# Later modulation chunks: every second one as float32 products with two moving columns on the tensor engine, the others by the vector engine alone

## The reference

```
silu_ctx = silu(c_ctx)[None]
silu_c = silu(c)
for l in range(2):
    sh_ap, sc_ap, gt_ap, sh_mp, sc_mp, gt_mp = split(silu_ctx @ ada_w[l] + ada_b[l], 6)
    sh_as, sc_as, gt_as, sh_ms, sc_ms, gt_ms = split(silu_c @ ada_w[l] + ada_b[l], 6)
    h = rms_norm(x, norm_mix_pre[l]) * (1 + sc_a) + sh_a
    ... mixer(h @ w_in[l]) ... gated residual with gt_a ... MLP with sh_m, sc_m, gt_m ...
```

## Time and profile before

| | us |
|---|---|
| three runs, median (lowest to highest) | 3354.6 (3351.59 to 3357.12) |
| the profiled execution, its own time | 3357.79 |
| its span, first to last instruction | 3356.1 |
| in-projection 0 beside the later chunks | about 113 to 403 of the span |
| mean granted TensorE clock over the span | 0.941 |

### The profile page before, as it was taken

How to read it: one execution, slowest core, us unless ns; L and a number is a source line. 1 busy time by engine, 2 the same in 40 slices (tenths; PEclk the granted TensorE clock), 3 DMA queues, 4 the chain that set the end, 5 groups by cost and what they waited for, 6 DMA issues and landing times.

```text
span 3356.1 us, 44680 instructions
## 1 busy us (share of the span) xinstructions
PE 3071.4 (92%) x17804; PEld 2687.3 (80%) x17804; DVE 1997.9 (60%) x2685; ACT 1183.4 (35%) x1884; POOL 1203.0 (36%) x705
## 2 busy tenths in 40 slices
PE   7999878999889999999998899857789999999998
PEld 3888646899768999978887898646668999988886
DVE  3699579555477644455555555477777644455555
ACT  2333234555453322211113476543253323211112
POOL 1466336100022544344341221145443544444341
PEclk9999979999899999999999999966689999999999
DMA  5565544000032232332521332321132232333421
GB/s 200 191 215 194 179 129 137 33 26 1 10 110 78 93 107 88 128 121 94 149 80 51 123 129 72 132 80 43 35 111 77 93 107 97 125 116 101 142 80 57
DMA packets 211326, 347.01 MB, mean 103 GB/s; under 512 B 18696, under 2 KB 110896, under 8 KB 211120
## 3 DMA queue, kind: packets, MB, share of 16 engines
q1 hardware_dynamic: 211120, 344.16, 30.8%
HBM read 259.18 MB, written 84.94 MB: 103 GB/s over the span
## 4 chain that ended last, share of the span: by engine, by line
PE 70%; DVE 15%; POOL 6%; issue 4%; ACT 3%; DMA 1%; SPq 1%; POOLq 1%; DVEq 0%; ACTq 0%
PE psum L1044 21%; PE psum L1022 17%; PE psum L692 6%; PE psum L2195 4%; PE psum L695 3%; DVE ada_acc L298 3%; PE psum L1368 3%; PE psum L2183 2%; PE psum L2190 2%; PE psum L2495 2%; DVE mix_x L2678 1%; PE psum L463 1%; DVE mix_v L2691 1%; PE psum L2841 1%; PE psum L1395 1%
## 5 line engine op out<-in xcount | busy, mean ns | idle before, releaser
L1044 PE MATMUL psum<-WF,H 128*128 128x512 f32 x3024 | 691.0, 391 | 11.2 <-POOL WF L1098 11.2
L1044 PEld LDWEIGHTS psum<-WF,H 128*128 128x128 f32 x3024 | 571.1, 189 | 130.7 <-POOL WF L1098 11.6
L1231 DVE TENSOR_TENSOR yacc<-yacc,psum 128x512 f32<-128x512 f32 x468 | 321.8, 688 | 314.7 <-PE psum L1044 314.7
L1022 PE MATMUL psum<-AT,w_slot 128*128 128x288 f32 x2688 | 366.0, 295 | 4.7 <-POOL w_slot L987 4.7
L1022 PEld LDWEIGHTS psum<-AT,w_slot 128*128 128x128 f32 x2688 | 359.5, 188 | 5.1 <-POOL w_slot L987 5.1
L1094 POOL TENSOR_TENSOR H<-pass_a,H 128x2304 fp32r<-128x2304 f32 x32 | 165.7, 5180 | 449.5 <-ACT H L1083 449.5
L692 PE MATMUL psum<-WT,AT 128*128 128x512 f32 (+1 forms) x1296 | 286.0, 381 | 4.2 <-ACT stage L738 4.2
L1083 ACT ACTIVATE H<-pass_a 128x2304 fp32r<-128x2304 f32 x32 | 68.2, 2132 | 596.8 <-PE psum L1044 573.2
L1022 PE MATMUL psum<-s_hi,w_slot 128*128 128x288 f32 x1344 | 269.1, 295 | 5.9 <-issue 4.3
L692 PEld LDWEIGHTS psum<-WT,AT 128*128 128x128 f32 x1296 | 234.4, 192 | 48.6 <-ACT stage L738 4.4
L628 POOL TENSOR_TENSOR WT<-RAW,WT 128x1024 fp32r<-128x1024 f32 (+3 forms) x34 | 114.8, 3401 | 346.3 <-ACT WT L617 346.3
(11 more groups left out here) (396 smaller groups left out, 5384.6 us busy)
## 6 DMA issues: line engine op xcount, KB each, us to landing
RAW<-ffn_w SPq DMA_DIRECT2D x64, 1024.0 KB, 6.3
ada_raw<-ada_w SPq DMA_DIRECT2D x18, 2048.0 KB, 8.2
pass_a<-hidden SPq DMA_DIRECT2D x64, 576.0 KB, 5.1
hidden<-hid SPq DMA_DIRECT2D x56, 576.0 KB, 3.3
RAW<-w_in_even SPq DMA_DIRECT2D x5, 2048.0 KB, 8.3
RAW<-w_in_odd SPq DMA_DIRECT2D x5, 2048.0 KB, 7.9
mix_x<-x_all SPq DMA_DIRECT2D x18, 512.0 KB, 3.6
feat_even<-stage SPq DMA_DIRECT2D x36, 256.0 KB, 5.1
```

What stands on the lines that cost most here:

```text
L1022: mm = nc.tensor.matmul(psum[:, bank + b, 0:HB], w_slot[p][:, w, k, :], TOKENS[p][x][:, k, b * HB:(b + 1) * HB], start=(begins and k == 0 ...
L1044: mm = nc.tensor.matmul(psum[:, DOWN_BANK[n % 8], :], H1[:, g % 2, a, m, (u // 2) * P:(u // 2 + 1) * P], w2[b][:, m, (u % 2) * 512:(u % 2 ...
L1231: tt(y, y, x, add).then_inc(dn_kept, 1)
```

## The change

Even slots and odd slots go different ways.

- **Odd slots** (1, 3, ..., 17): no DVE, ACT or POOL work on the block. PE takes the raw float32 weights themselves as the stationary operand, block by block of 128 x 128, and the two columns of `silu_c` (both vectors) as the moving one: 4 column blocks x 8 pieces = 32 float32 products with two moving columns, summed in PSUM.
- **Even slots** (0, 2, ..., 16): DVE does all eight pieces for both vectors, 16 instructions; PE makes the same 8 products with one column of ones as before.
- ACT's scaling and POOL's adding are gone, with their buffer and semaphores. `ada_acc` is now double-buffered over even slots.
- **Loads**: an odd block is loaded whole after PE's products of the odd slot before; an even block in two halves, each after DVE has read that half of the even slot before. `loads_at` places them in SP's list between the units' outputs, 0.68 of a 512-column unit behind the products of slot q - 2 for an odd slot, and 0.63 of a unit ahead of them and at them for the halves of an even one.
- DVE's order is: products of slot q (even), then `ada_keep` of q - 2 and q - 1.

The places of the products in PE's list stay as they were. The core of the diff:

```
+        def on_pe(q):
+            return q % 2 == 1
+
+        def ada_load(sp, q, h):
             l, at = slot_source(q)
-            sp.dma_start(slot_raw(q)..., ada_v[l][:, :, at:at + 512]).then_inc(ada_in[q % 2], 16)
+            rows = slot_raw(q).rearrange("p (k n) -> p k n", k=KD)
+            if on_pe(q):
+                sp.wait_ge(ada_sum[1], q // 2)
+                sp.dma_start(rows, ada_v[l][:, :, at:at + 512]).then_inc(ada_whole_in, 16)
+            else:
+                if q >= 2:
+                    sp.wait_ge(ada_part, 2 * KD * (q // 2 - 1) + KD * (h + 1))
+                sp.dma_start(rows[:, 4 * h:4 * h + 4, :], ada_v[l][:, 4 * h:4 * h + 4, at:at + 512]).then_inc(ada_in[h], 16)
 
         def ada_latent(dve, q):
+            e, raw = q // 2, slot_raw(q)
+            if e >= 2:
+                dve.wait_ge(ada_sum[0], e - 1)
+            for k in range(KD):
+                if k % 4 == 0:
+                    dve.wait_ge(ada_in[k // 4], 16 * (e + 1))
+                for who in range(2):
+                    acc, w, c = ada_acc[:, e % 2, who, :], raw[:, k * 512:(k + 1) * 512], silu_c[:, k, who:who + 1]
+                    if k:
+                        dve.wait_ge(ada_part, 2 * KD * e + 2 * k + who - 1)
+                        nc.vector.scalar_tensor_tensor(acc, w, c, acc, ALU.mult, ALU.add).then_inc(ada_part, 1)
+                    else:
+                        nc.vector.tensor_scalar(acc, w, c, None, ALU.mult).then_inc(ada_part, 1)
+
+        def ada_products(pe, q):
+            s, e = q % 2, q // 2
+            pe.wait_ge(ada_kept[s], e)
+            if on_pe(q):
+                pe.wait_ge(ada_whole_in, 16 * (e + 1))
+            else:
+                pe.wait_ge(ada_part, 2 * KD * (e + 1))
+            for m in range(4):
+                at = 256 + 2 * m
+                if on_pe(q):
+                    for k in range(KD):
+                        mm = nc.tensor.matmul(psum[:, 6 + s, at:at + 2], slot_raw(q)[:, k * 512 + m * P:k * 512 + (m + 1) * P], silu_c[:, k, :], start=(k == 0), stop=(k == KD - 1))
                 else:
+                    for who in range(2):
+                        mm = nc.tensor.matmul(psum[:, 6 + s, at + who:at + who + 1], ada_acc[:, e % 2, who, m * P:(m + 1) * P], ones[:, 0:1], start=True, stop=True)
             mm.then_inc(ada_sum[s], 1)
...
-        def ada_scalar(act, q, k):
-        def ada_gpsimd(pool, q):
...
+        def loads_at(c, u):
+            t0 = sum(unit_cost(cc) * units(cc) for cc in range(1, c)) + unit_cost(c) * u
+            t1 = t0 + unit_cost(c)
+            done = lambda q: FIRST_PRODUCT + PRODUCT_EVERY * (q - 2)
+            loads = [(done(q) + 370, q, 0) if on_pe(q) else (done(q) - 340 * (1 - h), q, h) for q in range(2, SLOTS) for h in range(1 if on_pe(q) else 2)]
+            return [(q, h) for t, q, h in sorted(loads) if t0 <= t < t1]
...
-            for q in range(SLOTS):
+            for q in range(0, SLOTS, 2):
                 ada_latent(dve, q)
                 if q:
+                    ada_keep(dve, q - 2)
                     ada_keep(dve, q - 1)
-            ada_keep(dve, SLOTS - 1)
+            for q in range(SLOTS - 2, SLOTS):
+                ada_keep(dve, q)
...
-                    for n in pieces_at(c, u):
-                        ada_scalar(act, n // (KD - K_DVE), K_DVE + n % (KD - K_DVE))
```

More of the change, by code:

```diff
@@ L138, in trunk @@
         ada_acc = Region(gate_row_at, AT0)("ada_acc", [P, 2, 2, 512])
-        ada_scaled = Region(SCR0 + 32 * K, END)("ada_scaled", [P, 2, 512])
         ATf = AT[:].bitcast(F32)
@@ L148, in trunk @@
         const_in, const_ready, silu_step, silu_ready = (sem_of(n) for n in ("const_in", "const_ready", "silu_step", "silu_ready"))
-        ada_in = [sem(f"ada_in{s}") for s in range(2)]
+        ada_in = [sem(f"ada_in{h}") for h in range(2)]
+        ada_whole_in = sem("ada_whole_in")
         ada_first_in = [sem_of(f"ada_first_in{r}") for r in range(4)]
         ada_part = sem("ada_part")
-        ada_begun = sem("ada_begun")
-        ada_scaled_ready = [sem(f"ada_scaled_ready{n}") for n in range(2)]
-        ada_added = [sem(f"ada_added{n}") for n in range(2)]
         ada_sum = [sem(f"ada_sum{s}") for s in range(2)]
@@ L262, in trunk @@
         SLOTS = 18
-        K_DVE = 3
         def slot_source(q):
@@ L270, in slot_raw @@
             return ada_raw[:, q % 2, :]
[L272 to L277, removed]
-            l, at = slot_source(q)
-            sp.dma_start(slot_raw(q).rearrange("p (k n) -> p k n", k=KD), ada_v[l][:, :, at:at + 512]).then_inc(ada_in[q % 2], 16)
-        def ada_latent(dve, q):
[L282 to L291, removed]
-                else:
[L293 to L300, removed]
@@ L302, in ada_uses @@
-        def ada_uses(q, k):
-            return (2, 3)[k % 2] * q + (k - K_DVE) // 2
-        def ada_scalar(act, q, k):
-            act.wait_ge(ada_in[q % 2], 16 * (q // 2 + 1))
-            act.wait_ge(ada_added[k % 2], ada_uses(q, k))
-            nc.scalar.activation(ada_scaled[:, k % 2, :], slot_raw(q)[:, k * 512:(k + 1) * 512], ACT.Copy, scale=silu_c[:, k, 1:2]).then_inc(ada_scaled_ready[k % 2], 1)
-        def ada_gpsimd(pool, q):
[L312 to L331, removed]
+        def on_pe(q):
+            return q % 2 == 1
@@ L742, in proj_scalar @@
                         lru_scalar(act, chain, units_before(c) + u)
-                        continue
-                    for n in pieces_at(c, u):
-                        ada_scalar(act, n // (KD - K_DVE), K_DVE + n % (KD - K_DVE))
         def proj_gpsimd(pool, l):
-            done = 0
             for c in range(1, N_GROUPS):
@@ L751, in proj_gpsimd @@
                     split_low(pool, 8 * l + c + 1, 4 if l else 1)
-                while l == 0 and done < pieces_at(c, units(c) - 1).stop // (KD - K_DVE):
-                    ada_gpsimd(pool, done)
-                    done += 1
         def proj_sync(sp, l):
-            loaded = 2
             if l == 0:
@@ L760, in proj_sync @@
                     sp.wait_ge(at_low[s], (5, 4)[s])
-                for q in range(2):
-                    ada_load(sp, q)
+                for q, h in ((0, 0), (0, 1), (1, 0)):
+                    ada_load(sp, q, h)
             for c in range(1, N_GROUPS):
@@ L786, in proj_sync @@
                             col_load(sp, n)
-                    while loaded < SLOTS and pieces_at(c, u).stop >= (KD - K_DVE) * (loaded - 1):
-                        ada_load(sp, loaded)
-                        loaded += 1
+                    for q, h in loads_at(c, u):
+                        ada_load(sp, q, h)
             if l:
```

## The result

The changed kernel takes 3427.39 us (median of 4 runs, 3424.51 to 3432.16) against 3354.4 in the same comparison: 1.0219 times as long, 95% interval 1.0201 to 1.0237. The forecast was 3430.6. The profiled execution has a span of 3422.8 us against 3356.1.

A forecast was written before the change was run, and what follows sets the result against it. PE was taken to bound in-projection 0. Waits gone (-20.3 us), thin products (+45.9) and the falling clock (+50.4) summed to +76.0, set on 3354.6 for 3430.6 us, with a range of 3376 to 3446.

The forecast's parts named there:

- PE sets the end of the stage: In-projection 0: PE, busy 274.5 of 293 us, bounds it; work added to its list lengthens the stage whole.
- Three waits go, 20.3 us: In-projection 0: PE's two waits for DVE and the 2.4 us one for ACT go, with their half clock: 20.3 us.
- the one of 4.2 us stays: In-projection 0: PE's wait for an ACT stage buffer, its output behind the next weights' load, remains at 4.2 us.
- Slot 2, the tight place: Start of group 2: SP, held until 168.4 us, may make DVE late; one wait of 1 to 4 us, costed at nothing.
- A product costs its weight block: Odd slots: each thin product takes 0.212 us whatever its columns, 6.8 us a slot, adding 45.9 us over nine.
- The clock falls in each odd slot: Odd slots: clock falls 3.7 us after the start, the remaining 3.1 us of work takes double, +3.1 us each.
- The wide products behind lose 2.5 us each: Units behind each odd slot: wide products begin at half clock, costing 2.5 us a slot.
- The two terms for odd slots: Odd slots: 45.9 us for the thin products and 50.4 us for the falling clock, wide products behind included.
- rival 1: Odd slots: the busy thin run holds the clock, so only 25.6 us are added, time 3380; chance 0.13.
- rival 2: In-projection 0: the 20.3 us of waits stay, up to 3451 with a low clock; chance 0.05.
- rival 3: Odd slots: thin products are cheap, 0.106 us each giving 3350 or 0.080 giving 3342; chance 0.02.
- The signs: Profile after: odd slots 9 to 11 us, DVE busy some 104 us, in-projection 0 longer by 70 to 80 us.

The follow-up runs named there:

- short odd slots: Changed kernel with 4 products (k = 0 only) in place of 32 in each odd slot, work left out: 3340.11 us, 0.9954 of the kernel before.
- the pieces: Changed kernel with each odd slot's 32 thin products in four runs of 8, 3385.21 us, or two runs of 16, 3414.18 us.
- the two kernels in which it holds: Changed kernel with 64 moving columns in place of 2, 3382.75 us, and with the thin products in four runs of 8, 3385.21 us.
- all-DVE kernel with the earlier products: All 18 slots go the even way, with products first at 2200, every 1120, in place of 2760 and 1080: 3342.24 us, 0.9963 of the kernel before.

## Why the prediction was right, point by point

- **PE sets the end of the stage, and what is put in its list comes out at the end whole.** Right: 71.6 us by PE's own rows, 70.3 at the stage's last product, 73.0 between the medians, 66.7 between the spans. In the profiled execution the rest of the program is 3.6 us shorter; its instructions are the same there, and I take that for the scatter between executions, which was not tested.
- **Three waits go, 20.3 us; the one of 4.2 us stays.** Right, with 4.1 left. The reason was right in its first half: DVE alone takes 0.75 us per product. The rest was costed at nothing too easily. With short odd slots the new load order brings 12.6 us of waits and half clock of its own. Slot 2, the tight place that I named and left out of the sum, was the largest of them (3.27 us, in my 1 to 4). In the changed kernel DVE ended slot 2 at 180.2 us and PE came for it at 186.7, between my 184 and 189.
- **A product costs its weight block: 0.212 us, 6.8 us an odd slot.** The mechanism is right: a run of 32 at full clock comes to 7.07 us with 2 columns, by the pieces, and to 7.06 with 64, measured. The size is a little low. 0.212 is a mean over a run of 8, and 16 in a row show that each further one costs 0.223, the upper bound that attention's products gave. The blocks of nine odd slots add 9 x (7.06 - 1.70) = 48.2 us, where the sum had 45.9.
- **The clock falls in each odd slot, 3.7 us after its start.** It fell in all nine, 2.2 to 5.5 us after the start, 3.9 on average. The thin part cost 89.3 - 9 x 7.06 = 25.8 us above full clock, where the sum had 27.9. That 3.7 came so close is in part luck. It is the middle of 2.9 and 4.4, the ends of a stretch of the stall before 236.2 us, and this window of the kernel before shows that the clock was down at 2.9 already:

```profile
234.80:236.20 1.40, 0.00 (x0) 0.01 (x1) 1.40 (x3) 0.00 (x0) 0.72 (x1) 0.50 0.00 0
```

With 2.9 the same sum gives 3.9 + 2.5 = 6.4 us for an odd slot and 3438 us. A stall told that the clock would fall, but not well when.
- **The wide products behind lose 2.5 us each.** A term mis-sized: 1.32 to 2.83, together 17.9 and not 22.5. The two rows I took it from stood behind a wait and a thin run that had begun at half clock; whether that is why was not tested.
- **The sum.** The two terms for odd slots made 45.9 + 50.4 = 96.3, and PE's rows show 91.9: blocks 2.3 more, the thin part's clock 2.1 less, the wide products' 4.6 less. The first two cancel, which is luck too. The 3 us between forecast and result are the rest of this and the scatter of the medians.
- **The rivals.** The clock does not hold (rival 1): its price of 3380 is that of the two kernels in which it holds, 3383 and 3385. The waits did go (rival 2), and a thin product is not cheap (rival 3).
- **The signs.** The odd slots took 8.5 to 11.5 us where I named 9 to 11, DVE was busy 109.6 us in the stage and not 104, and the stage is 70.8 us longer, within 70 to 80.

In sum, of the 92 us that PE got, 48 are weight blocks and 44 are the clock's cost. The first part alone is more than the 20.3 us that went. With the clock held the change would still be a loss, of 26 to 28 us.

## What to carry to other kernels

Before work goes to the tensor engine, count its weight blocks and not its columns: 32 products of two columns cost as much as 32 of 64, and a reduction that DVE can make first leaves only 8. Where a thin run can't be avoided, keep it short between wide products (1.7 us held here, 3.5 us not always), or give it more columns, which were free up to 64: here either saved over 40 us of 3427. And where two engines are both near full, ask which one the last one to finish waits for, then look at what stands behind a waiting instruction in the sync engine's list: moving two weight loads behind two to four outputs was worth 11 to 12 us, after moving the one ahead of them alone had shown no gain, as the next hold took its place.

## What the runs showed of the hardware that was not expected

- Streaming 64 columns in place of 2 made the kernel 44.6 us faster, at 7.06 us per odd slot against 8.5 to 11.5.
- DVE's products of two SBUF operands don't only slow down beside POOL, they stand still: 14 of them take 9.36 us without POOL and 18.11 us beside one `split_low` of 9.21 us, so 8.75 more, nearly its whole length. One of them alone took 9.50 us, where the median is 0.74. In the all-DVE kernel with the earlier products:

```profile
265.38 9.36 DVE L284 SCALAR_TENSOR_TENSOR ada_acc<-ada_raw,silu_c,ada_acc 128x512 f32<-128x512 f32 x14
...
277.57 18.11 DVE L284 SCALAR_TENSOR_TENSOR ada_acc<-ada_raw,silu_c,ada_acc 128x512 f32<-128x512 f32 x14
```

```profile
279.29 9.21 POOL L592 TENSOR_TENSOR WT<-RAW,WT 128x4096 fp32r<-128x4096 f32 x1 [47.39 <-ACT WT L581]
```

Lowest, median and longest of these products in ns:

```profile
L284 DVE SCALAR_TENSOR_TENSOR ada_acc<-ada_raw,silu_c,ada_acc x252: 732/741/9498, 131.1 to 372.7; 128x512 f32<-128x512 f32 x126
```

The Trainium skill's "SBUF — State Buffer", section "SBUF: two separate sides", says that the port pair which the two engines share is held for a whole instruction and the other one is blocked fully. The product of 9.50 us agrees. The 18.6 us of the earlier trace rows fit it as well: seven products alone are 5.3 us, the `split_low` beside them 9.15, and POOL's additions, which ran beside them too, leave room for the other 4.
